# Norm outputs transposed by SyncE DMA, a state chain with one step per chunk, one pre-added LayerNorm sum, x and out on SyncE, and the last column half per token tile

## The chip, the cores and the metric

The kernel runs on the 8 cores of one Trainium2 chip. Each core works on 2 of the 16 sequences; nothing is exchanged between cores. The metric is the device time of the slowest core in microseconds (us). Engine names: PE is TensorE (matmul), DVE is VectorE, ACT is ScalarE, POOL is GpSimd, SP is SyncE, which here only issues DMAs.

## The reference

One decoder layer on 2064 tokens a sequence (16 meta tokens, then 2048), width 1024, feed-forward width 2816:

```
u = rms_norm(h) @ w_in                  # conv value 512, conv gate 512, q 256, k 256, v 512, out-gate 512, low rank 16
v = c_val * sigmoid(c_gate);  y = causal depthwise conv of v (width 31) + b
y_conv = silu(layer_norm over the 512 channels(y))
log_a = logsigmoid(lr @ w_gate2 + b) / 16;  bc = cumsum of log_a in a chunk
scores = tril((q e^bc) (k e^-bc)^T);  kv = (k e^(b_last - bc))^T v
state = e^b_last * state + kv                              # one step per chunk
o = scores v + (q e^bc) state_before;  y_gla = rms_norm per head(o) * silu(g)
h = h + concat(y_conv, y_gla) @ w_out
h = h + (silu(n @ w_gate) * (n @ w_up)) @ w_down           # n = rms_norm(h)
out = rms_norm(h), meta positions dropped
```

## The kernel before

**Blocks and stages.** A core's 4096 tokens are 8 blocks of 512, each of 4 token tiles of 128. A block goes through `mixer` (norm, projections, conv, attention, w_out, second norm) and `ffn` (22 pairs j of gate and up matmuls, two column halves of 6 down steps, the final norm). The mixer of block b+1 is merged into the ffn of block b, so the program is: mixer 0 alone (with a pass over the meta tokens), seven merged stages, ffn 7 alone. In this document a stage starts with the first matmul on `x2T` of an ffn; that moment is called T0.

**Norm and transposition.** `norm` (L554) writes a normed tile to one of two buffers `xn_tm` [128 tokens x 1024]: an ACT Square with a sum (L557), eight small DVE instructions (L525 to L534) and one DVE multiplication (L560). `transp` (L565) turns it to channel-major form: 8 PE transpositions of 128x128 into one PSUM bank (L572) and one ACT copy (L575) to `xT` (for the mixer) or `x2T` (for the ffn). The next norm into the same `xn_tm` waits for these transpositions.

**LayerNorm sums.** The mean over 512 channels is 4 fp32 matmuls with a matrix of ones (L744), the sum of squares 4 bf16 ones (L750). The difference and product that apply it are POOL instructions (L864, L865).

**State.** For each of the 4 chunks of a block POOL writes two halves of `Rbd` from the state `S` (L940), then DVE computes `U` (L946, 2 instructions) and the new `S` (L950, 2).

**Weights.** 48 tiles [128 x 2048]. At its first use a tile is loaded and cast from fp32 by a POOL DMA (`wring<-wpack`, L420), and SP stores the bf16 copy (`wsc<-wring`, L421); later uses load that copy on SP (`wring<-wsc`, L417). Slots wring0 to wring3 serve the mixer, wring4 to wring7 the ffn. A slot's next load is issued once PE has used the tile in it. The shifted copies for the conv (`rep<-vT`, L679) are 32 SP DMAs a block. x and the meta tile are loaded, and out is stored, by POOL DMAs (L457, L459, L601, L1130). `h` has two sets of 4 tiles; the load of x into a set waits until the out DMA of the block two before has read it.

**The order.** `Prog.add` records every instruction with its buffers; `Prog.schedule` (L139) simulates the engines with the costs of `Meter` and one DMA channel of rate `DMA_RATE`, and emits each engine's list in that order. An engine, and SP's and POOL's queue too, then runs its list in order: what waits holds everything behind it.

## Time and profile before

| | us |
|---|---|
| median of 3 runs (1739.64 to 1741.36) | 1740.09 |
| the profiled execution | 1738.95 |
| its slowest core, first to last instruction (span) | 1737.4 |
| spans of the 8 cores | 1726.5 to 1737.4 |
| PE busy | 1538.3 (89%) |
| DVE, ACT, POOL busy | 845.8, 526.2, 192.9 |
| mean granted TensorE clock, this core | 0.963 |

The profiled execution is 1.55 us longer than its span, and 1.1 us below the median. By the window table the span falls into 174 us of mixer 0 (PE busy for 95.6), the first merged stage from 174 to 400 (its weights are loaded for the first time), six stages of 195 to 197 us, and ffn 7 with the end. Matmul durations in rows are longer than the interval at which they follow each other, because they are pipelined: the start times of rows tell the interval.

### The profile page before, as it was taken

The numbers are of one execution on the slowest core, as the hardware profiler recorded it, in microseconds if no ns is written. First come the engines' busy times: TensorE is split into PE (matmuls) and PEld (weight loads), VectorE is DVE, ScalarE is ACT, GpSimd is POOL, SyncE is SP. The second block draws the span as 40 slices with busy tenths as digits, with TensorE's granted clock in tenths as the row PEclk, the third lists the DMA queues.
The fourth block names the chain that finished last, engine by engine and source line by source line (L and its number), as shares of the span: only waits on it lengthen the run. The fifth ranks groups of instructions, "written<-read, shape, count | busy, mean of one in ns | idle before, by whom it ended". The sixth has DMA issues, their size and how long they took to land.

```text
span 1737.4 us, 27522 instructions; the slowest of 8 cores (1726.5 to 1737.4 us)
## 1 busy us (share of the span) xinstructions
PE 1538.3 (89%) x8498; PEld 711.8 (41%) x8498; DVE 845.8 (49%) x1950; ACT 526.2 (30%) x822; POOL 192.9 (11%) x262
## 2 busy tenths in 40 slices
PE   1676997878899989999899989999899989999993
PEld 1332443433344434444444434444444434444431
DVE  4246427603427554466427554466427554466322
ACT  2233343201342234313342234313342234313101
POOL 2040013001002000200012000200002000200000
PEclk9897999999999999999999999999999999999997
DMA  9963786798353474445654475435653464434541
GB/s 211 230 150 98 160 194 153 171 213 272 103 147 122 169 220 144 150 144 165 193 156 122 169 218 142 153 134 174 196 154 122 170 218 144 151 122 140 176 145 73
DMA packets 93487, 281.92 MB, mean 162 GB/s; under 512 B 12576, under 2 KB 29344, under 8 KB 93344
## 3 DMA queue, kind: packets, MB, share of 16 engines
q1 hardware_dynamic: 76928, 220.84, 40.0%
q0 software_dynamic: 16416, 59.32, 15.5%
q8 instruction: 72, 1.18, 0.3%
q14 instruction: 71, 0.58, 0.1%
HBM read 245.70 MB, written 41.94 MB: 166 GB/s over the span
## 4 chain that ended last, share of the span: by engine, by line
PE 73%; DVE 8%; DMA 7%; issue 6%; ACT 2%; SPq 2%; DVEq 1%; POOL 0%; ACTq 0%; POOLq 0%
PE ps L581 49%; PE ps L1106 14%; PE ps L726 3%; DMA h_0<-xin 2%; DMA wring<-wpack 2%; PE ps L572 2%; SPq L679 2%; PE ps L744 2%; DVE xn_tm L560 1%; DMA wsc<-wring 1%; PE ps L639 1%; DVE y_tm L1000 1%; DVE stn L532 1%; DMA h_3<-pre 1%; DVE stn L534 1%
## 5 line engine op out<-in xcount | busy, mean ns | idle before, releaser
L581 PE MATMUL ps<-x2T,wring 128*128 128x512 bf16 x2816 | 646.7, 387 | 19.8 <-DVE ftmp L1088 9.1
L581 PEld LDWEIGHTS ps<-x2T,wring 128*128 128x128 bf16 x2816 | 274.8, 100 | 365.2 <-issue 62.0
L1106 PE MATMUL ps<-wring,actT 128*128 128x512 bf16 x1408 | 319.8, 382 | 20.5 <-DMA wring<-wpack 9.7
L1088 DVE SCALAR_TENSOR_TENSOR ftmp<-ftmp,ps 128x512 f32<-128x512 f32 x176 | 120.1, 686 | 257.1 <-ACT ftmp L1087 250.7
L1106 PEld LDWEIGHTS ps<-wring,actT 128*128 128x128 bf16 x1408 | 135.9, 98 | 182.2 <-issue 30.6
L1087 ACT ACTIVATE ftmp<-ps 128x512 f32<-128x512 f32 x176 | 104.7, 595 | 288.8 <-PE ps L581 232.8
L581 PE MATMUL ps<-xT,wring 128*128 128x512 bf16 x768 | 171.7, 380 | 2.6 <-DVE vT L668 1.1
L1090 DVE SCALAR_TENSOR_TENSOR actT<-ftmp,ps 128x512 bf16<-128x512 f32 x176 | 119.7, 686 | 74.7 <-PE ps L581 70.8
L581 PE MATMUL ps<-wring,xT 128*128 128x512 bf16 x512 | 120.2, 386 | 2.8 <-ACT actT L712 1.4
L581 PE MATMUL ps<-wring,yT 128*128 128x512 bf16 x512 | 118.6, 382 | 2.7 <-ACT yT L1015 2.7
L572 PE MATMUL ps<-ident,xn_tm 128*128 128x128 bf16 x520 | 45.6, 239 | 80.8 <-DVE stn L525 38.7
L581 PEld LDWEIGHTS ps<-xT,wring 128*128 128x128 bf16 x768 | 74.7, 98 | 92.1 <-issue 4.6
L940 POOL TENSOR_TENSOR Rbd<-S,emid 64x256 bf16<-64x256 f32 x64 | 43.0, 671 | 473.7 <-ACT emid L781 345.1
L572 PEld LDWEIGHTS ps<-ident,xn_tm 128*128 128x128 bf16 x520 | 36.9, 107 | 100.1 <-issue 94.1
L581 PEld LDWEIGHTS ps<-wring,xT 128*128 128x128 bf16 x512 | 50.3, 99 | 65.9 <-issue 9.8
L581 PEld LDWEIGHTS ps<-wring,yT 128*128 128x128 bf16 x512 | 49.9, 98 | 61.9 <-issue 4.7
L1114 DVE TENSOR_TENSOR h_0<-h_0,ps 128x512 f32<-128x512 f32 x16 | 11.0, 688 | 124.7 <-PE ps L1106 124.7
L1130 POOL DMA_DIRECT2D out<-h_0 x8 | 4.7, 588 | 554.4 <-DVE h_0 L1127 554.4
L672 DVE SCALAR_TENSOR_TENSOR vT<-mtmp,ps 128x512 bf16<-128x512 f32 x32 | 22.0, 688 | 81.5 <-issue 49.1
L726 PE MATMUL ps<-rep,wcv 128*32 128x512 bf16 x1024 | 59.3, 380 | 0.5 <-issue 0.2
L575 ACT ACTIVATE x2T<-ps 128x1024 bf16<-128x1024 bf16 x32 | 32.4, 1023 | 83.2 <-PE ps L572 80.4
L970 ACT ACTIVATE sg<-ps 128x512 f32<-128x512 f32 x32 | 19.1, 597 | 126.5 <-PE ps L581 90.8
(181 smaller groups left out, 1383.0 us busy)
## 6 DMA issues: line engine op xcount, KB each, us to landing
wring<-wsc SPq DMA_DIRECT2D x336, 512.0 KB, 4.3
wring<-wpack POOLq DMA_DIRECT2D x48, 512.0 KB, 9.5
wsc<-wring SPq DMA_DIRECT2D x48, 512.0 KB, 6.9
rep<-vT SPq DMA_DIRECT2D x256, 67.5 KB, 3.4
h_0<-xin POOLq DMA_DIRECT2D x8, 512.0 KB, 12.5
h_1<-xin POOLq DMA_DIRECT2D x8, 512.0 KB, 10.3
h_2<-xin POOLq DMA_DIRECT2D x8, 512.0 KB, 11.5
h_3<-xin POOLq DMA_DIRECT2D x8, 512.0 KB, 12.5
```

Of the source, the lines that this page charges most:

```text
L572: ins = e.transpose(out=ptb[:, kc, :], in_=xn_tm[i][:, kc * 128:(kc + 1) * 128], identity=ident[:])
L575: P.add("act", lambda e: e.activation(out=dst, in_=ptb, func=AF.Copy), R=[Bpt], W=[Bdst])
L581: ins = e.matmul(pt_ap, lhsT=lhs(kc), rhs=rhs(kc), start=(kc == 0), stop=(kc == KC - 1))
L672: P.add("dve", lambda e, pv=pv, th=th: e.scalar_tensor_tensor(out=vT[:, c, 32:32 + T], in0=th[:], scalar=1.0, in1=pv[:], op0=ALU.add, op1= ...
L679: P.add("sp", lambda e, s_=s_, g=g, c0=c - 1: e.dma_start(out=rep[s_ * 32:(s_ + 1) * 32, c0:c0 + 2, g, :], in_=vT[g * 32:(g + 1) * 32, c0: ...
L726: ins = e.matmul(pcv[g * 32:(g + 1) * 32, :], lhsT=wcv[:, c, g, a, :], rhs=rep[:, c, g, 4 * a:4 * a + T], start=(a == 0), stop=(a == 7))
L744: ins = e.matmul(p1[:], lhsT=ones[:], rhs=ycv[c], start=(c == 0), stop=(c == 3))
L940: P.add("pool", lambda e, t=t, hh=hh, rows=rows: e.tensor_tensor(out=Rbd[rows, t, :, hh, :], in0=S[rows, :, :], in1=em2[rows, :, t].unsque ...
L1087: P.add("act", lambda e: e.activation(out=th[:], in_=pg[:], func=AF.Tanh, scale=0.5), R=[Bpg], W=[Bth])
L1088: P.add("dve", lambda e: e.scalar_tensor_tensor(out=th[:], in0=th[:], scalar=1.0, in1=pg[:], op0=ALU.add, op1=ALU.mult), R=[Bpg, Bth], W=[ ...
L1090: P.add("dve", lambda e: e.scalar_tensor_tensor(out=actT[:, j, :], in0=th[:], scalar=0.5, in1=pu[:], op0=ALU.mult, op1=ALU.mult), R=[Bpu, ...
L1106: ins = e.matmul(ps[t][:], lhsT=actT[:, j, t * 128:(t + 1) * 128], rhs=wd3[:, j - 4 * s_, :], start=(j == 0), stop=(j == NJ - 1))
```

## The change

- `transp` becomes one SP instruction, `dma_start_transpose` from `xn_tm` to `xT` or `x2T` (now laid out tile by tile); the PE transpositions, their PSUM bank and the ACT copy go.
- The LayerNorm mean: three POOL additions, then one fp32 matmul.
- The state: `S` has 5 slots; 4 multiplications (two halves at once) and 8 chained steps on DVE, then the 8 `Rbd` writes. The cumulative sums are 8 scans of 128 in place of 2 of 512.
- x, meta tile and out move from POOL's queue to SP's; the first four mixer weights are issued after x tiles 0 and 3 have landed; two gain vectors are loaded later.
- The down steps are one entry per token tile; in the last ffn the second column half runs token tile by token tile, each with its final norm and store, and 4 of its 6 weights lie in the mixer's slots.
- The planner's DMA rate goes from 185e3 to 380e3 bytes per us with a latency of 3.0 in place of 2.0. It sets no hardware, but moves instructions on every engine.

```diff
-DMA_RATE = 185e3
+DMA_RATE, DMA_LAT = 380e3, 3.0
...
+            if name == "dma_start_transpose":
+                self.nbytes += n * o.shape[0] * 3
+                self.cost += 0.5
...
-                end = dma_free + 2.0
+                end = dma_free + DMA_LAT
...
-            P.add("pool", lambda e: e.dma_start(out=h[1][3][:], in_=pre_d), W=[Bh[1][3]], dkey="h1_3")
+            P.add("sp", lambda e: e.dma_start(out=h[1][3][:], in_=pre_d), W=[Bh[1][3]], dkey="h1_3")
             for t in range(NT):
-                P.add("pool", lambda e, t=t: e.dma_start(out=h[0][t][:], in_=xin[t * 128:(t + 1) * 128, :]),
+                P.add("sp", lambda e, t=t: e.dma_start(out=h[0][t][:], in_=xin[t * 128:(t + 1) * 128, :]),
...
-                        wissue(r, n)
+                        wissue(r, n, [Bh[0][0]] if r == 0 and n < 2 else [Bh[0][3]] if r == 0 else [BxT[3]])
...
             def transp(i, dst, Bdst):
-                pt, Bpt = mps()
-                ptb = pt[:].bitcast(BF16).rearrange("p (k n) -> p k n", k=KC)
-
-                def tr(e):
-                    ins = None
-                    for kc in range(KC):
-                        ins = e.transpose(out=ptb[:, kc, :], in_=xn_tm[i][:, kc * 128:(kc + 1) * 128], identity=ident[:])
-                    return ins
-                P.add("pe", tr, R=[Bxn[i], Bident], W=[Bpt])
-                P.add("act", lambda e: e.activation(out=dst, in_=ptb, func=AF.Copy), R=[Bpt], W=[Bdst])
+                P.add("sp", lambda e: e.dma_start_transpose(dst, xn_tm[i][:]), R=[Bxn[i]], W=[Bdst], dkey=f"xt{i}")
...
-                            P.add("pool", lambda e, t=t: e.dma_start(out=h[hs][t][:], in_=xin[row0 + t * 128:row0 + (t + 1) * 128, :]),
+                            P.add("sp", lambda e, t=t: e.dma_start(out=h[hs][t][:], in_=xin[row0 + t * 128:row0 + (t + 1) * 128, :]),
...
-                    def mm1(e):
-                        ins = None
-                        for c in range(4):
-                            ins = e.matmul(p1[:], lhsT=ones[:], rhs=ycv[c], start=(c == 0), stop=(c == 3))
-                        return ins
...
+                    P.add("pool", lambda e: e.tensor_tensor(out=mu[:], in0=ycv[0], in1=ycv[1], op=ALU.add), R=Bycv[0:2], W=[Bmu])
+                    P.add("pool", lambda e: e.tensor_tensor(out=rs[:], in0=ycv[2], in1=ycv[3], op=ALU.add), R=Bycv[2:4], W=[Brs_])
+                    P.add("pool", lambda e: e.tensor_tensor(out=mu[:], in0=mu[:], in1=rs[:], op=ALU.add), R=[Brs_], W=[Bmu])
+                    P.add("pe", lambda e: e.matmul(p1[:], lhsT=ones[:], rhs=mu[:], start=True, stop=True), R=[Bmu, Bc], W=[Bp1])
+                    P.add("pe", mm2, R=Bysq + [Bc], W=[Bp2])
...
+                        sp4 = sp.rearrange("p a (t n) -> p (a t) n", n=128)
+                        for i in range(2 * nt):
+                            P.add("dve", lambda e, i=i: e.tensor_tensor_scan(
+                                out=cs4[:, i, :], data0=ones[:], data1=sp4[:, i, :], initial=0.0,
...
+                    el = csb[:].rearrange("p a (t n) -> p a t n", n=128)[:, :, :, 127]
+                    P.add("dve", lambda e: e.tensor_tensor(out=dec[:], in0=em2, in1=el, op=ALU.mult), R=[Bemid, Bcs], W=[Bdec])
+                    for t in range(NT):
+                        P.add("dve", lambda e, t=t: e.tensor_tensor(
+                            out=S[:, sl[t + 1]], in0=pkv[t // 2][0][:, (t % 2) * 256:(t % 2) * 256 + 256].rearrange(
+                                "p (a n) -> p a n", a=2), in1=el[:, :, t].unsqueeze(2).to_broadcast([128, 2, 128]), op=ALU.mult),
+                            R=[Bcs, pkv[t // 2][1]], W=[BS[sl[t + 1]]])
+                    for t in range(NT):
+                        for hp in range(2):
+                            P.add("dve", lambda e, t=t, hp=hp: e.scalar_tensor_tensor(
+                                out=S[:, sl[t + 1], hp, :], in0=S[:, sl[t], hp, :], scalar=dec[:, hp, t:t + 1],
+                                in1=S[:, sl[t + 1], hp, :], op0=ALU.mult, op1=ALU.add), R=[BS[sl[t]], Bdec], W=[BS[sl[t + 1]]])
                     for t in range(NT):
                         for hh in range(2):
                             rows = slice(hh * 64, (hh + 1) * 64)
                             P.add("pool", lambda e, t=t, hh=hh, rows=rows: e.tensor_tensor(
-                                out=Rbd[rows, t, :, hh, :], in0=S[rows, :, :],
+                                out=Rbd[rows, t, :, hh, :], in0=S[rows, sl[t], :, :],
                                 in1=em2[rows, :, t].unsqueeze(2).to_broadcast([64, 2, 128]), op=ALU.mult),
-                                R=[BS, Bemid], W=[BR[t]])
-                        for hp in range(2):
-                            o = (t % 2) * 256 + hp * 128
-                            P.add("dve", lambda e, t=t, hp=hp, o=o: e.scalar_tensor_tensor(
-                                out=U[:, hp, :], in0=S[:, hp, :], scalar=em2[:, hp, t:t + 1], in1=pkv[t // 2][0][:, o:o + 128],
-                                op0=ALU.mult, op1=ALU.add), R=[BS, Bemid, pkv[t // 2][1]], W=[BU])
-                        for hp in range(2):
-                            P.add("dve", lambda e, t=t, hp=hp: e.tensor_scalar(
-                                out=S[:, hp, :], in0=U[:, hp, :], scalar1=csb[:, hp, t * 128 + 127:t * 128 + 128], scalar2=None,
-                                op0=ALU.mult), R=[BU, Bcs], W=[BS])
...
+                def down_mm(e, wd, t, js, j0):
+                    wd3 = wd[:].rearrange("p (j n) -> p j n", j=4)
+                    ins = None
+                    for j in js:
+                        ins = e.matmul(ps[t][:], lhsT=actT[:, j, t * 128:(t + 1) * 128], rhs=wd3[:, j - j0, :],
+                                       start=(j == 0), stop=(j == NJ - 1))
+                    return ins
...
+                            for t in range(NT):
+                                P.add("pe", lambda e, t=t: down_mm(e, wd, t, js_of(s_), 4 * s_),
+                                      R=[Bwd] + [Bact[j] for j in js_of(s_)], W=[Bps[t]])
+                                if s_ == 5:
...
+                def stat(t):
+                    i = nxt("xn", 2)
+                    P.add("act", lambda e: e.activation(out=xn_tm[i][:], in_=h[hs][t][:], func=AF.Square, accum_out=stf[:, 0, t:t + 1]),
+                          R=[Bh[hs][t]], W=[Bxn[i], Bstf[t]])
+
+                def finish(t0, t1):
+                    y = newton_row([stf[:, k, t0:t1] for k in range(6)], Bstf[t0:t1], 1.0 / D, RMS_EPS)
+                    for t in range(t0, t1):
+                        ht, Bht = h[hs][t], Bh[hs][t]
+                        P.add("dve", lambda e, t=t, ht=ht: e.scalar_tensor_tensor(
+                            out=ht[:], in0=ht[:], scalar=y[:, t - t0:t - t0 + 1], in1=gfin[:], op0=ALU.mult, op1=ALU.mult),
+                            R=[Bht, Bstf[t], Bgain[id(gfin)]], W=[Bht])
+                        P.add("sp", lambda e, t=t, ht=ht: e.dma_start(out=out[orow0 + t * 128:orow0 + (t + 1) * 128, :], in_=ht[:]),
+                              R=[Bht], dkey=f"h{hs}_{t}")
 
                 def final():
                     for t in range(NT):
+                        stat(t)
+                    finish(0, NT)
+
+                def down_last():
+
+                    wds = [wget(W_FD + 6 + s_, r=0 if s_ < NWM else 1)[0] for s_ in range(6)]
                     for t in range(NT):
+                        for s_ in range(6):
+                            wd, Bwd = wds[s_]
+                            P.add("pe", lambda e, t=t, s_=s_, wd=wd: down_mm(e, wd, t, js_of(s_), 4 * s_),
+                                  R=[Bwd] + [Bact[j] for j in js_of(s_)], W=[Bps[t]])
+                        h_add(1, t)
+                        stat(t)
+                        finish(t, t + 1)
+                units.append((19.0, down_last) if last else (0.0, final))
```

PE, the rows before the first projection of a stage, where `xn_tm` 0 and 1 are the normed tiles, `ps0` to `ps3` the ffn's PSUM banks and `ps4` to `ps7` the mixer's. Before:

```order
L581 MATMUL ps3<-x2T,wring7 128x512 x8
L581 MATMUL ps0<-x2T,wring4 128x512 x8
L581 MATMUL ps2<-x2T,wring4 128x512 x8
L572 MATMUL ps7<-ident,xn_tm1 128x128 x8
L581 MATMUL ps1<-x2T,wring5 128x512 x8
L581 MATMUL ps3<-x2T,wring5 128x512 x8
L572 MATMUL ps4<-ident,xn_tm0 128x128 x8
L581 MATMUL ps0<-x2T,wring6 128x512 x8
L581 MATMUL ps5<-xT,wring0 128x512 x8
```

PE at the same place now, from the last down steps of the ffn before to the low-rank projection (buffer numbers left out):

```order
L1093 MATMUL ps<-wring,actT 128x512 x40
L572 MATMUL ps<-x2T,wring 128x512 x216
L572 MATMUL ps<-xT,wring 128x512 x64
L626 MATMUL ps<-xT,wgl 32x512 x8
L572 MATMUL ps<-x2T,wring 128x512 x8
```

The eight groups of transpositions of a stage are gone from PE's list (four stood between these x2T matmuls, four in the w_out part); in most stages 216 matmuls on x2T now stand ahead of the first one on xT.

POOL, the out stores and the x loads of a stage (`h1_0` to `h1_3` are the four tiles of one set). Before:

```order
L1130 DMA out<-h1_2 128x1024 [waits sem_dve]
L1130 DMA out<-h1_3 128x1024 [waits sem_dve]
L601 DMA h1_0<-xin 128x1024 [waits dsem_h1_0]
L601 DMA h1_1<-xin 128x1024 [waits dsem_h1_1]
L601 DMA h1_2<-xin 128x1024 [waits dsem_h1_2]
L601 DMA h1_3<-xin 128x1024 [waits dsem_h1_3]
L940 TENSOR_TENSOR Rbd<-S,emid 64x2x128 [waits sem_act,sem_pool,sem_pe]
```

SP at this place now (`dsem_h1_0` is the store of that tile, `sem_pe` a tile used, `sem_dve` the end of a DVE instruction):

```order
L1126 DMA out<-h1_3 128x1024 [waits sem_dve]
L420 DMA wring6<-wsc 128x2048 [waits dsem_wh6,sem_pe]
L595 DMA h1_0<-xin 128x1024 [waits dsem_h1_0]
L595 DMA h1_1<-xin 128x1024 [waits dsem_h1_1]
L420 DMA wring7<-wsc 128x2048 [waits dsem_wh7,sem_pe]
L595 DMA h1_2<-xin 128x1024 [waits dsem_h1_2]
L595 DMA h1_3<-xin 128x1024 [waits dsem_h1_3]
L420 DMA wring4<-wsc 128x2048 [waits dsem_wh4,sem_pe]
L420 DMA wring5<-wsc 128x2048 [waits dsem_wh5,sem_pe]
L566 DMA_TRANSPOSE xT<-xn_tm1 128x8x128 [waits sem_dve,dsem_xt1]
```

The stores, loads and transposes now stand in one list with the ffn's weight loads. Between the four transposes of xT stand the weights of one pair each, so that the second, third and fourth come after a pair of loads that waits for PE.

SP at the start of the program (wring4 to wring7 hold the first ffn weights, `actT` receives the meta tile here). Before:

```order
L448 DMA gng<-gla_norm_g 128x1
L421 DMA wsc<-wring0 128x2048 [waits dsem_wp0]
L421 DMA wsc<-wring1 128x2048 [waits dsem_wp1]
L421 DMA wsc<-wring2 128x2048 [waits dsem_wp2]
L679 DMA rep<-vT 32x2x540 [waits sem_dve]
```

Now:

```order
L424 DMA wsc<-wring4 128x2048 [waits dsem_wp4]
...
L424 DMA wsc<-wring7 128x2048 [waits dsem_wp7]
L566 DMA_TRANSPOSE actT<-xn_tm0 128x8x128 [waits sem_dve]
L595 DMA h1_3<-xin 128x1024 [waits dsem_h1_3,sem_act]
L566 DMA_TRANSPOSE xT<-xn_tm1 128x8x128 [waits sem_dve]
L424 DMA wsc<-wring0 128x2048 [waits dsem_wp0]
...
L424 DMA wsc<-wring3 128x2048 [waits dsem_wp3]
L566 DMA_TRANSPOSE xT<-xn_tm0 128x8x128 [waits sem_dve]
```

The first transposes stand behind the stores of wring4 to wring7, the transposes of tiles 1 to 3 also behind those of wring0 to wring3, and each store waits for its fp32 load.

## Rows read from the trace of the kernel before

**Rows 1.** Window table: the first merged stage and a later one.

```profile
core 1: us, PE busy (x) PEld busy (x) DVE busy (x) ACT busy (x) POOL busy (x), PEclk, DMA share, GB/s
174.00:400.00 226.00, 193.84 (x1040) 87.82 (x1038) 92.62 (x215) 59.07 (x91) 32.52 (x47) 0.96 0.79 181
889.00:1084.00 195.00, 187.33 (x1028) 86.94 (x1030) 103.76 (x239) 64.62 (x101) 20.49 (x25) 0.98 0.51 162
```

**Rows 2.** Groups of one stage (885 to 1081 us): busy, mean ns | idle before, releaser.

```profile
L572 PE MATMUL ps<-ident,xn_tm 128*128 128x128 bf16 x64 | 5.7, 241 | 4.5 <-DVE stn L525 4.2 <-DVE xn_tm L560 0.2
...
L864 POOL TENSOR_TENSOR rep<-rep,mtmp 128x512 f32<-128x512 f32 x4 | 5.1, 1270 | 17.1 <-PE ps L750 16.7
...
L575 ACT ACTIVATE x2T<-ps 128x1024 bf16<-128x1024 bf16 x4 | 4.1, 1022 | 12.2 <-PE ps L572 12.2
L744 PE MATMUL ps<-rep,ones 128*128 128x512 f32 x8 | 3.6, 592 | 0.0
...
L946 DVE SCALAR_TENSOR_TENSOR U<-S,emid,ps 128x128 f32<-128x128 f32 x8 | 2.8, 344 | 0.9 <-PE ps L931 0.4
```

**Rows 3.** Timeline of PE, start of a stage: start us, us, instruction [idle before].

```profile
1001.37 13.97 PE L581 MATMUL ps<-x2T,wring 128*128 128x512 bf16 x64 [0.94 <-DVE h_0 L1114]
...
1034.34 1.01 PE L572 MATMUL ps<-ident,xn_tm 128*128 128x128 bf16 x8 [4.20 <-DVE stn L525]
1035.15 3.62 PE L581 MATMUL ps<-x2T,wring 128*128 128x512 bf16 x8
...
1055.03 13.98 PE L581 MATMUL ps<-xT,wring 128*128 128x512 bf16 x64
```

**Rows 4.** Timeline of PE, end of the stage before that.

```profile
990.10 1.25 PE L572 MATMUL ps<-ident,xn_tm 128*128 128x128 bf16 x16
...
998.09 0.61 PE L572 MATMUL ps<-ident,xn_tm 128*128 128x128 bf16 x8
998.54 1.89 PE L1106 MATMUL ps<-wring,actT 128*128 128x512 bf16 x8
```

**Rows 5.** Timeline of DVE there: the last normed tile for x2T.

```profile
994.94 1.28 DVE L560 SCALAR_TENSOR_TENSOR xn_tm<-h_3,stn,gffn 128x1024 bf16<-128x1024 f32 x1
```

**Rows 6.** Timeline of POOL, the first store of out in that stage.

```profile
1012.42 0.60 POOL L1130 DMA_DIRECT2D out<-h_0  x1 [69.96 <-DVE h_0 L1127]
```

**Rows 7.** DMA issues of the program: queue, count, KB, median us to landing.

```profile
wring<-wsc SPq DMA_DIRECT2D x336, 512.0 KB, 4.3
...
wsc<-wring SPq DMA_DIRECT2D x48, 512.0 KB, 6.9
rep<-vT SPq DMA_DIRECT2D x256, 67.5 KB, 3.4
h_0<-xin POOLq DMA_DIRECT2D x8, 512.0 KB, 12.5
...
out<-h_0 POOLq DMA_DIRECT2D x8, 512.0 KB, 4.2
...
out<-h_3 POOLq DMA_DIRECT2D x8, 512.0 KB, 9.6
```

**Rows 8.** Timelines of PE (first transposition), SP and ACT at the program's start.

```profile
20.11 1.01 PE L572 MATMUL ps<-ident,xn_tm 128*128 128x128 bf16 x8 [20.11 <-DVE stn L525]
...
25.80 7.11 SPq L421 DMA_DIRECT2D wsc<-wring  x3
...
41.52 1.02 ACT L575 ACTIVATE xT<-ps 128x1024 bf16<-128x1024 bf16 x1 [2.28 <-PE ps L572]
```

**Rows 9.** Timelines of PE, ACT, DVE and POOL at the program's end.

```profile
1688.05 20.84 PE L1106 MATMUL ps<-wring,actT 128*128 128x512 bf16 x88 [2.73 <-DVE h_3 L1114]
...
1713.57 1.06 ACT L1121 ACTIVATE xn_tm<-h_3 128x1024 bf16<-128x1024 f32 x1
...
1717.26 1.28 DVE L1127 SCALAR_TENSOR_TENSOR h_0<-h_0,stf,gfin 128x1024 f32<-128x1024 f32 x1
...
1722.95 0.54 POOL L1130 DMA_DIRECT2D out<-h_3  x1 [0.92 <-DVE h_3 L1127]
```

More of the change, by code:

```diff
@@ L352, in build @@
             Bst = [Buf(f"st{i}") for i in range(2 * NT)]
-            Bstf = Buf("stf")
+            Bstf = [Buf(f"stf{t}") for t in range(NT)]
             Bsto = [Buf(f"sto{i}") for i in range(2)]
@@ L583, in mm8, with mixer @@
                 return f
-            def mixer(hs, row0, first, meta, load):
+            def mixer(bi, row0, first, meta, load):
+                hs = bi % 2
                 units = []
+                s0 = (NT * bi) % (NT + 1)
+                sl = [(s0 + i) % (NT + 1) for i in range(NT + 1)]
                 def unit(cost):
@@ L1066, in _, with ffn @@
                     def _(t=t):
-                        transp(xni2[t], x2T[:, :, t * 128:(t + 1) * 128], Bx2T[t])
+                        transp(xni2[t], x2T[:, t], Bx2T[t])
                 return units
-            def ffn(hs, orow0):
+            def ffn(hs, orow0, last):
                 units = []
```

163 lines of the change are left out of this document (66 added, 97 removed).

## Prediction

> **What bounds the kernel now.** I read the busy shares by window first [rows 1], then the groups of one stage [rows 2], then PE's timeline at both ends of a stage [rows 3, 4], the DMA issues [rows 7], and the program's two ends [rows 8, 9]. In a later stage PE is busy for 187.33 of 195 us and DVE for 103.76: PE is the bound, and only 7.7 us are waits. A matmul of 128x512 counts 0.216 us there: 64 of them take 13.98 and 8 take 1.89, and the 56 between cost 12.09 [rows 3, 4]. The largest wait, 4.20 us, stands before the first transposition to xT [rows 3]. So a stage gets shorter by what leaves PE's list and by that wait, as long as no transfer that takes their place is late. The first merged stage is another matter: 226 us with 32 idle, DMA engines busy for .79 of it [rows 1], because weights are read in fp32 and written back there.
>
> The profiled execution took 1738.95 us (span 1737.4 and 1.55 outside), 1.1 below the median. I sum against 1738.95 and add the 1.1 at the end.
>
> **What a stage loses.** Transpositions: eight groups of 8. The one of 1034.34 is followed by x2T matmuls at 1035.15, so it takes 0.81 [rows 3]; the one of 998.09 takes 0.45 [rows 4]. Two of the first kind and six of the second: 4.3 us. The 4.20 us wait goes with them [rows 3]. LayerNorm mean: the group of eight fp32 records is 3.6 us for four matmuls [rows 2] (each is two passes); one in place of four leaves a quarter, which saves 2.6. Together 11.1 us of 195.
>
> **What a stage gains in waits.** All of them hang on L, the time from a transpose's issue on SP to its landing. No row of before shows a transpose by DMA. The nearest rows are SP's own: 3.4 us for 67.5 KB, 4.3 for a weight load of 512 KB, 6.9 for a store of 512 KB; out's slowest store takes 9.6 and x's slowest load 12.5, both on POOL's queue [rows 7]. A transposed tile is 256 KB from SBUF to SBUF on SP, so I take 4.3, with 3.4 and 6.9 as likely ends and 12.5 as the far one.
>
> - x2T. The last tile for it is normed at 994.94 + 1.28 = 996.22 [rows 5]; the transposition before it, whose two groups stand after the last w_out matmul, began at 990.10 [rows 4], 6.1 earlier. By the order now only 40 down matmuls, 8.6 us, stand between w_out and x2T. PE waits 6.1 + 0.1 (issue) + L - 8.6 = L - 2.4, which is 1.9 us. Before, the last 8 down matmuls ended at 998.54 + 8 x 0.216 = 1000.27 and x2T began at 1001.37: 1.1 [rows 3, 4]. Cost 0.8.
> - xT. In the order now 216 x2T matmuls precede the first on xT, so it is due at T0 + 46.7; before it was T0 + 53.7 (1055.03 less 1001.37). The last of the four transposes stands on SP behind a pair of weights whose slots come free when the sixth pair has been used, at 6 x 32 x 0.216 = T0 + 41.5. It lands at about T0 + 41.9 + L = 46.2; with L = 6.9 PE waits 2.1. I take 1.
> - Weights. SP runs its list in order. The load of wring7 now stands behind a load of x, which waits until the store of the same tile has landed. Stores begin about T0 + 11 (1012.42 less 1001.37) [rows 6], the second a DVE instruction later, T0 + 12.2, and land 4.2 to 9.6 later [rows 7]. The weights are next needed at T0 + 13.8 plus a load's slack: a pair feeds 32 matmuls, 6.9 us, and a load takes 4.3, which leaves 2.6, and one pair is held ahead. That gives 0 to 3.7 us of idle PE there, and up to 0.9 more at the load behind the fourth x. I take 2, of 0 to 4.6. On POOL the same waits held no weights.
>
> The other edits I cost at nothing. Three POOL additions of 1.27 us (L864) [rows 2] stand before the LayerNorm matmul, but x2T matmuls of the merged ffn fill PE meanwhile; without that cover about 2.6 us a stage. The state chain on DVE drops the U instructions (eight of 344 ns [rows 2]) for twelve of such size, on an engine 53% busy; uncovered, 1.4 us. The ACT copies of 1.02 us [rows 2] go from an engine that is a third busy. The planner's new rate sets no hardware; what it moves is in the three orders above, and was counted.
>
> So a later stage nets 11.1 - 0.8 - 1 - 2 = 7.3 us, and six of them 44. In the first merged stage the fp32 loads set much of the pace; I give it 4 (0 to 11).
>
> **The end.** PE ended at 1688.05 + 20.84 = 1708.89, the span at 1737.4: 28.5 us [rows 9]. The final norm's first multiplication started 8.4 us after PE, at 1717.26, behind four Squares of 1.06, and the last store was issued at 1722.95 [rows 9]. Now one tile is left: 8.4 less three Squares, 5.2; the multiplication 1.28; one store of 4.2 to 9.6 [rows 7], and about 1 to finish: 12 to 17, where I take 14.5, a gain of 14. The 2.73 us wait between the column halves [rows 9] should lose some 2. Together 16 (11 to 19).
>
> **The start.** Before, the first transposition ran at 20.11 and xT was complete at 41.52 + 1.02 = 42.5 [rows 8]. Now SP holds the first transposes behind the stores of wring4 to wring7, and tiles 1 to 3 also behind those of wring0 to wring3. The first three stores were issued from 25.80 to 32.91 [rows 8], about 3.6 apart; eight at this pace end at 50.6. With x ahead of the weights and L behind, xT is complete at 44 to 56: a loss of 1.5 to 13. Part of it returns, since mixer 0 is not PE's to set. I take 3 lost, of 8 gained to 13 lost.
>
> Sum: 44 + 4 + 16 - 3 = 61, so 1738.95 - 61 = 1678, on the scale of the medians **1679 us**. Own range: 1655 to 1705, from L at 3.4 with no weight late, to L = 5.5 with 3 us of late weights a stage and 9 us lost at the start.
>
> **The rivals.**
>
> *All of it is covered* (L = 3.4 or less, no weight late). Seven stages give 11.1 each, 78; the end 19, the start -1.5: 95 less, 1645. For it: one pair of weights is held ahead, and the DMA share of a later stage is only .51 [rows 1]. Against it: the four SP lists above put waits in front of loads that were free of them.
>
> *SP's queue eats the gain.* With L = 6.9 x2T costs 4.5 - 1.1 = 3.4, xT 2.1, weights 4.6: a stage keeps 11.1 - 10.1 = 1. Seven of these, the end 11, the start -11: 7 less, 1733. For it: SP now carries 16 DMAs a stage more, and its stores take 6.9 [rows 7]. Moving x and out alone then bought nothing. An x load of 512 KB took 12.5 us on POOL's queue, a weight load of that size 4.3 on SP's [rows 7], but they ran in different company. The Trainium skill ("DMA: Bandwidth & Descriptors", section "Issuing engines are not separate DMA queues") says that DMAs of all engines end up on the same 16 DMA engines, and that the choice of issuer saves only the time of issuing; by that rule x stays at 12.5 on SP. No run here shows it yet.
>
> *Slower: the transposes land late.* The mechanism is at the stage's start. Only two xn_tm buffers exist, so the third norm waits for the first transpose to land; tiles follow each other in 24 matmuls, 5.2 us, so above that L counts twice: x2T costs (L - 2.4) + (L - 5.2) - 1.1, xT L - 4.8, weights 2. At L = 9.6, the slowest store [rows 7], that is 10.5 + 4.8 + 2 = 17.3 against 11.1: each of seven stages is 6.2 longer, 43; the ends give back 13; 30 more, 1770. It decides from L of about 8. For it: a transpose moves 2-byte elements in a pattern that no row shows. Against it: 256 KB is half of every tile in the rows. The Trainium skill ("VectorE: DVE Perf Modes", section "The three transpose paths") gives 1309 ns for a DMA transposition of 128x128 against 390 on TensorE; eight in a row would be an estimate of 10.5 us for L, and by the same formula about 1788. TensorE's eight took 0.45 to 0.81 us here [rows 3, 4], far below eight times 390, since they are pipelined; how far a DMA's are, no row here shows.
>
> **How the numbers follow.** Chances: the forecast .52, all covered .20, gain eaten .18, slower .10. A difference under 0.2%, 3.5 us, can't be told from none. The forecast and "all covered" are faster by more; of "gain eaten" about .10 is faster, .05 within the bound, and .03 slower, which with the last rival makes faster .82, same .05, slower .13. The range of 8 in 10 leaves out little at either side: 1643 to 1735.
>
> **What would show it.** The landing time of the transposes (4.3); PE's waits before the first x2T matmul (1.9) and the first xT matmul (0 to 2) of a stage, and before the x2T matmuls of the second and third pair (2); a later stage of about 188 us with no 4.2 us wait; an end of 14.5 us after PE; xT of mixer 0 complete at 44 to 56. The forecast is wrong if the transposes take over 6 us, if PE waits over 5 us a stage for a weight tile behind an out store, or if the POOL additions show up as a wait before the LayerNorm matmul.

## The result, and the profile after

The changed kernel takes 1668.34 us (median; before 1740.72 beside it), a ratio of 0.9590, 95% interval 0.9560 to 0.9619. The forecast was 1679, so the size and the sign came out. Most of the reasons did not: the largest single gain belongs to an edit that the prediction priced at nothing, and the edit that it was built on, the transposes by DMA, costs time in the whole.

The profiled execution took 1674.6 us (span 1673.1 on core 0); the one of before 1738.95 (core 1). Executions of the changed kernel scatter more than those of before, over 9 us (1665.61 to 1674.6) against 2, and the profiled one is the longest of its four. Both spans, cut where an ffn begins (T0: the first matmul on x2T):

| stretch | before | after | difference | forecast |
|---|---|---|---|---|
| mixer 0, to the first T0 | 173.9 | 202.6 | +28.7 | +3 |
| first merged stage | 229.1 | 202.0 | -27.0 | -4 |
| second | 207.2 | 190.6 | -16.6 | -7.3 |
| five later ones | 977.8 | 945.2 | -32.6 (6.5 each) | -36.5 (7.3 each) |
| last T0 to the end | 149.5 | 132.7 | -16.8 | -16 |

The later stages and the end came in sum as worked out. The start lost ten times its term, and the first two merged stages, where little was expected, returned all of it and 15 us more. The second merged stage of before had been counted ahead of the prediction among the six of 195 to 197 us; it took 207.2.

PE's timeline of after (start us, us, instruction, idle before), at the starts of the program, of the first and the second ffn, and of a later stage; it answers to [rows 3, 4, 8]:

```profile
54.37 5.28 PE L572 MATMUL ps<-actT,wring 128*128 128x128 bf16 x48 [54.37 <-DMA actT<-xn_tm]
71.01 12.00 PE L572 MATMUL ps<-xT,wring 128*128 128x512 bf16 x48 [11.36 <-DMA xT<-xn_tm]
...
202.58 12.77 PE L572 MATMUL ps<-x2T,wring 128*128 128x512 bf16 x48 [18.57 <-DMA x2T<-xn_tm]
...
404.62 12.44 PE L572 MATMUL ps<-x2T,wring 128*128 128x512 bf16 x48 [3.94 <-DMA x2T<-xn_tm]
...
784.45 12.25 PE L572 MATMUL ps<-x2T,wring 128*128 128x512 bf16 x56 [1.90 <-DMA x2T<-xn_tm]
797.41 10.52 PE L572 MATMUL ps<-x2T,wring 128*128 128x512 bf16 x48 [0.72 <-DVE actT L1079]
811.33 18.87 PE L572 MATMUL ps<-x2T,wring 128*128 128x512 bf16 x79 [3.40 <-DMA wring<-wsc]
```

In the later stage PE waits 1.90 us for x2T (forecast 1.9), nothing for xT (forecast 1), and 3.40 for a weight tile (forecast 0 to 4.6). At the program's start the first matmul waits until 54.37 and the first on xT runs at 71.01, where before it ran at 42.69; the first ffn then waits 18.57 for its x2T.

The window table of that stage against the later one of [rows 1] (columns as there), and the DMA issues that answer to [rows 7]:

```profile
784.45:973.20 188.75, 180.57 (x971) 81.98 (x980) 104.19 (x242) 57.64 (x93) 20.10 (x20) 0.99 0.62 180
```

```profile
wring<-wsc SPq DMA_DIRECT2D x336, 512.0 KB, 4.5
...
h_0<-xin SPq DMA_DIRECT2D x8, 512.0 KB, 7.4
...
h_3<-xin SPq DMA_DIRECT2D x8, 512.0 KB, 10.5
out<-h_0 SPq DMA_DIRECT2D x8, 512.0 KB, 5.8
...
xT<-xn_tm SPq DMA_TRANSPOSE x32, 5.1
...
x2T<-xn_tm SPq DMA_TRANSPOSE x32, 4.2
...
actT<-xn_tm SPq DMA_TRANSPOSE x1, 18.9
```

L, which no row of before showed, is 4.2 and 5.1 us in the median, where 4.3 was taken. But the meta tile's transpose at the start took 18.9.

### The profile page after: what moved, and what is told of

It reads as the page before. It is cut to its first block, busy times and chain, and to the rows that moved or that the text cites. A ratio compares the mean times of both kernels' runs of the same rounds, so it can differ in the third digit from the quotient of the medians.

```text
span 1673.1 us, 26740 instructions; the slowest of 8 cores (1636.5 to 1673.1 us)
## 1 busy us (share of the span) xinstructions
PE 1473.3 (88%) x7864; PEld 670.7 (40%) x7930; DVE 853.4 (51%) x1998; ACT 464.8 (28%) x757; POOL 189.8 (11%) x221
## 4 chain that ended last, share of the span: by engine, by line
PE 68%; DMA 13%; DVE 8%; issue 5%; SPq 3%; ACT 1%; DVEq 0%; POOL 0%; ACTq 0%; POOLq 0%
PE ps L572 51%; PE ps L1093 11%; PE ps L720 3%; DMA wring<-wpack 2%; DMA x2T<-xn_tm 2%; DMA out<-h_1 2%; SPq L673 2%; DMA wring<-wsc 2%; DVE y_tm L989 1%; DMA actT<-xn_tm 1%; DMA h_1<-xin 1%; DVE xn_tm L560 1%; PE ps L633 1%; DMA rep<-vT 1%; DVE sto L984 1%
## 5 line engine op out<-in xcount | busy, mean ns | idle before, releaser
L1093 PE MATMUL ps<-wring,actT 128*128 128x512 bf16 x1382 | 315.3, 380 | 5.5 <-DMA wring<-wpack 4.2
L572 PEld LDWEIGHTS ps<-xT,wring 128*128 128x128 bf16 x768 | 75.0, 98 | 104.9 <-issue 16.6
L572 PE MATMUL ps<-actT,wring 128*128 128x128 bf16 x80 | 8.1, 284 | 66.6 <-DMA actT<-xn_tm 54.4
L423 POOL DMA_DIRECT2D wring<-wpack x48 | 26.1, 546 | 279.0 <-PE ps L572 170.8
L656 ACT ACTIVATE mtmp<-ps 128x512 f32<-128x512 f32 (+1 forms) x36 | 20.2, 561 | 99.7 <-PE ps L572 86.6
L557 ACT ACTIVATE xn_tm<-h_0 128x1024 bf16<-128x1024 f32 x16 | 16.9, 1056 | 107.3 <-DVE h_0 L1045 87.6
L989 DVE SCALAR_TENSOR_TENSOR y_tm<-ps,sto,sg 128x128 bf16<-128x128 f32 x128 | 42.0, 349 | 8.1 <-DVE sto L550 0.4
## 6 DMA issues: line engine op xcount, KB each, us to landing
h_3<-xin SPq DMA_DIRECT2D x8, 512.0 KB, 10.5
```

What stands on the lines that cost most here:

```text
L423: P.add("pool", lambda e: e.dma_start(out=dst, in_=wpack[tile]), R=after, W=[B_], dkey=f"wp{sl}")
L572: ins = e.matmul(pt_ap, lhsT=lhs(kc), rhs=rhs(kc), start=(kc == 0), stop=(kc == KC - 1))
L656: P.add("act", lambda e, pg=pg, th=th, n=n: e.activation(out=th[:, 0:n], in_=pg[:, 0:n], func=AF.Tanh, scale=0.5), R=[Bpg], W=[Bth])
L989: P.add("dve", lambda e, hd=hd, hsl=hsl: e.scalar_tensor_tensor(out=y_tm[i][:, hsl], in0=po[:, hsl], scalar=y[:, hd:hd + 1], in1=sg[i][:, ...
L1093: ins = e.matmul(ps[t][:], lhsT=actT[:, j, t * 128:(t + 1) * 128], rhs=wd3[:, j - j0, :], start=(j == 0), stop=(j == NJ - 1))
```

## The experiments

All ratios are to the kernel before on the same chip; "us" behind a ratio is the ratio times 1740.7. By this the changed kernel is at 1669.

### e1: the planner's numbers alone

```diff
-DMA_RATE = 185e3
+DMA_RATE, DMA_LAT = 380e3, 3.0
-                self.nbytes += n * o.shape[0] * (2 if kw["in_"].dtype == BF16 else 4)
+                self.nbytes += n * o.shape[0] * (2 if kw["in_"].dtype == BF16 else (4 if o.dtype == F32 else 5.4))
-                end = dma_free + 2.0
+                end = dma_free + DMA_LAT
```

> The kernel before with only the planner's new numbers (rate 380e3, latency 3.0, bytes of a cast load). Theory A (the gain of a later stage comes from what leaves PE's list: transpositions, their wait, three fp32 matmuls): the six later stages stay at 195 us, all within 5 us of 1740.7. Theory B (the gain comes from the order that the new numbers make): stages of about 189, some 1700 or below.

0.9681 (0.9658 to 0.9705), 1685 us: three quarters of the whole gain, with no instruction added or removed. Theory B was right on the sum and wrong on the place: T0 stood at 176.0, 368.1 and 561.5 on core 0, so the first merged stage took 192.1 us (229.1 before) and the second 193.4 (207.2), while five later stages averaged 195.0 (195.6 before; over all eight cores 192.6 and 195.1). How this comes about is read at the end of the first merged stage. First PE of the kernel before, from 385 us on, then PE of e1 from 335 us on:

```profile
385.90 3.61 PE L1106 MATMUL ps<-wring,actT 128*128 128x512 bf16 x16 [2.48 <-DMA wring<-wpack]
390.32 3.61 PE L1106 MATMUL ps<-wring,actT 128*128 128x512 bf16 x16 [0.80 <-DMA wring<-wpack]
394.19 3.61 PE L1106 MATMUL ps<-wring,actT 128*128 128x512 bf16 x16 [0.26 <-DMA wring<-wpack]
400.03 1.89 PE L1106 MATMUL ps<-wring,actT 128*128 128x512 bf16 x8 [2.22 <-DMA wring<-wpack]
```

```profile
335.30 1.89 PE L1106 MATMUL ps<-wring,actT 128*128 128x512 bf16 x8
337.03 3.62 PE L581 MATMUL ps<-wring,yT 128*128 128x512 bf16 x16
340.48 3.62 PE L1106 MATMUL ps<-wring,actT 128*128 128x512 bf16 x16
343.94 1.89 PE L581 MATMUL ps<-wring,yT 128*128 128x512 bf16 x8
345.66 3.62 PE L1106 MATMUL ps<-wring,actT 128*128 128x512 bf16 x16
```

Before, only down steps (L1106) are left, and each waits for its fp32 weight tile; the mixer's work is used up. In e1 w_out (yT) and down steps alternate, and none waits. The window tables, before and e1, of the two ends and of the whole first merged stage:

```profile
350.00:402.90 52.90, 39.53 (x170) 16.25 (x169) 3.29 (x6) 0.60 (x2) 4.23 (x8) 0.97 1.00 228
174.00:402.90 228.90, 195.72 (x1048) 88.54 (x1047) 93.43 (x217) 59.09 (x92) 32.52 (x47) 0.96 0.80 184
```

```profile
330.00:368.00 38.00, 36.76 (x200) 17.57 (x197) 18.04 (x46) 9.62 (x14) 2.12 (x4) 1.00 1.00 249
176.00:368.00 192.00, 187.50 (x1048) 86.91 (x1048) 94.81 (x217) 59.52 (x91) 32.40 (x47) 0.99 0.94 221
```

At both ends the DMA engines are full (1.00). Before, PE was busy for 39.5 of 52.9 us and DVE for 3.3; in e1 36.8 of 38.0 and 18.0. In the order made for the lower rate the w_out matmuls ran from 302 to 326 us and the down steps came last; in e1 w_out runs from 326 to 356, between them. Over the whole stage the DMA engines were busy for 0.80 of the time before and 0.94 in e1, and the last fp32 tile landed at 399.9 and at 359.1.

The end is not all of the 37 us. PE was idle for 33.2 us of the stage before, in e1 for 4.6. Of the 33.2 us 9.7 were waits for fp32 tiles, the others mostly waits of 1 to 3 us for the mixer's own steps on DVE, which e1's order covers. The remaining 8 us are PE's busy time (195.7 and 187.5), for the same matmuls at a mean granted clock of 0.96 and 0.99. In the second merged stage no fp32 tile is left to load; there idle time fell from 15.9 to 7.3 us. That the moved order is the cause follows from the run, since nothing else differs; which of the three numbers did it was not tried.

### e2: TensorE's transpositions back; e6: the transposes by DMA alone on e1

e2 is the changed kernel with the eight PE transpositions and the ACT copy of a tile again; e6 is e1 with the transposes by DMA.

```diff
-                P.add("sp", lambda e: e.dma_start_transpose(dst, xn_tm[i][:]), R=[Bxn[i]], W=[Bdst], dkey=f"xt{i}")
+                P.add("pe", tr, R=[Bxn[i], Bident], W=[Bpt])
+                P.add("act", lambda e: e.activation(out=dst, in_=ptb, func=AF.Copy), R=[Bpt], W=[Bdst])
```

> The changed kernel with the norm outputs transposed by TensorE and copied by ACT again, everything else as changed. Theory A: a later stage is 4.3 us longer by the transpositions and 1 to 4 by the wait before those of xT, less the 2 us wait for x2T, so 189 becomes 193 to 196, and the whole 1668 plus 7 x 3 to 7, 1690 to 1717. Theory B: the order pays, not the transposes: 1668 within 5. The start should be shorter (no transposes behind stores on SP), with T0 of the first ffn some 20 us earlier than 202; if that is worth its length, the sum is 20 less.

> The kernel before with the planner's new numbers (as e1) and the transposes by DMA, nothing else. If the transposes by DMA are a loss in sum as e2 says (about 17 us): 1700 to 1710 beside e1's 1687, with the first T0 at 195 to 205 against 176. If they shorten a later stage by what leaves PE (4.3 us and the waits): later stages 187 to 190 against e1's 195, first T0 late all the same, 1665 to 1685.

e2: 0.9485 (0.9470 to 0.9500), 1651 us, 18 less than the changed kernel: both theories missed, since without the part that was to bring the gain the kernel is faster. e6: 0.9857 (0.9838 to 0.9877), 1716 us, 31 more than e1: undoing the edit and doing it alone agree in sign. On the slowest core e6 has its first T0 at 211.3 (e1 176.0) and a first merged stage of 206.6 (192.1); its five later stages average 191.9 (195.0). So the transposes by DMA give 3 us in a later stage of that kernel (over eight cores 4.2: 188.4 for 192.6) and lose 50 in the first two stretches. In the first merged stage PE of the changed kernel waits 11.6 us for fp32 weight tiles and 3.9 for x2T; in e2, with TensorE's transpositions, it waits for neither DMA there, and the stage takes 188.3 us for 202.0. PE of e2 at the start and in a later stage:

```profile
45.92 1.01 PE L572 MATMUL ps<-ident,xn_tm 128*128 128x128 bf16 x8 [15.13 <-DVE cvec L507]
...
64.37 5.83 PE L581 MATMUL ps<-xT,wring 128*128 128x512 bf16 x18 [1.49 <-ACT xT L575]
...
761.51 13.98 PE L581 MATMUL ps<-x2T,wring 128*128 128x512 bf16 x64
775.78 13.97 PE L581 MATMUL ps<-x2T,wring 128*128 128x512 bf16 x64 [0.30 <-DVE ftmp L1086]
792.13 1.89 PE L581 MATMUL ps<-x2T,wring 128*128 128x512 bf16 x8 [2.38 <-DMA wring<-wsc]
793.86 0.61 PE L572 MATMUL ps<-ident,xn_tm 128*128 128x128 bf16 x8
794.30 3.62 PE L581 MATMUL ps<-x2T,wring 128*128 128x512 bf16 x16
```

At the start its first matmul on xT runs at 64.37, also late: the second group of transpositions waits 15.13 us for DVE, which waits for small constants (read below, at e3). In the later stage a transposition takes 0.44 us and nothing waits ahead of it: the 4.20 of [rows 3] is gone with PE's transpositions in place, and a wait of 2.38 stands before, at a weight tile. There is no wait for x2T. Its five later stages average 189.4 us on core 0, after's 189.0; over the eight cores 188.4 and 187.0, a difference no larger than that between two profiles of the same PE order (see e8).

### e3 and e5: another start

```diff
+            gain(gmix, g_mix_d, "gm")           # and the small constants: ahead of x on SP
...
-                        wissue(r, n, [Bh[0][0]] if r == 0 and n < 2 else [Bh[0][3]] if r == 0 else [BxT[3]])
+                    wissue(0, n, [Bh[0][0]] if n < 2 else [Bh[0][3]])
...
+                if i == 1 + NT and wseq is not None:      # after the transposes of xT of block 0
+                    for f_ in late:                       # the first four bf16 stores
+                        f_([BxT[3]])
+                    for n in range(RING[1][1]):           # the first ffn weights
+                        wissue(1, n, [BxT[3]])
```

The changed kernel makes the loads of the ffn weights depend on the last tile of xT, but at that place of the program nothing has written it yet, so that no wait arises and these four are the first weights to be loaded. Here they come after xT.

> The changed kernel with another start: the small constants and gmix before x on SP, the loads of wring4 to wring7 and the first bf16 stores after the four transposes of the first xT. Theory A (the 28.7 us that the first ffn starts later are lost time): T0 of the first ffn at 175 to 185 instead of 202, and the whole 1640 to 1650. Theory C (the first loads of the weights, fp32 with their stores, set when the second ffn can start, so the late start is given back): T0 of the second ffn stays at 395 to 405, and the whole is 1660 to 1670.

> TensorE's transpositions as in e2, and the other start of e3: constants and gmix before x on SP, the loads of wring4 to wring7 and the first bf16 stores after the first xT. With TensorE's transpositions nothing of the first xT stands behind those stores, so T0 of the first ffn should be 173 to 178 (e1: 176; e2: 190). Theory A (a late start is lost time): the second T0 at 362 to 368 and the whole 12 to 14 below e2, 1638 to 1640. Theory C (the first loads of the weights set the second T0): it stays at 375 to 380, the whole at 1648 to 1653.

e3, with transposes by DMA: 0.9585 (0.9543 to 0.9628), no difference from the changed kernel; neither theory was tested, for T0 stayed at 203.7. e5, with TensorE's: 0.9404 (0.9386 to 0.9423), 1637 us, 14 less than e2; T0 172.8 to 179.1 on the eight cores, the second at 361 to 371. It beats both kernels: 6.0% below before, 1.9% below the change. Theory A holds: a late start is lost time, as soon as it can be mended. With the transposes by DMA this start did not mend it. SP of the changed kernel, at the start:

```profile
19.87 15.42 SPq L424 DMA_DIRECT2D wsc<-wring  x4
35.38 14.70 SPq L566 DMA_TRANSPOSE actT<-xn_tm  x1
50.25 0.45 SPq L595 DMA_DIRECT2D h_3<-xin  x1
50.79 2.44 SPq L566 DMA_TRANSPOSE xT<-xn_tm  x1
53.32 3.19 SPq L424 DMA_DIRECT2D wsc<-wring  x4
```

Until 35.29 SP waits for the four fp32 loads, as forecast; but then it is held for 14.70 us by the issue of one transpose (1.2 us in a later stage), while the DMA engines are full (busy for all of the time from 35 to 54 us). DVE at the same time:

```profile
25.90 1.28 DVE L560 SCALAR_TENSOR_TENSOR xn_tm<-h_3,stn,gmix 128x1024 bf16<-128x1024 f32 x1 [14.34 <-DMA gmix<-norm_mix_g]
...
44.30 0.17 DVE L505 TENSOR_SCALAR gb<-gb 128x2 f32<-128x2 f32 x1 [17.12 <-DMA gng<-gla_norm_g]
44.48 1.28 DVE L560 SCALAR_TENSOR_TENSOR xn_tm<-h_0,stn,gmix 128x1024 bf16<-128x1024 f32 x1
```

gmix and a constant of half a KB, now issued behind x, hold DVE until 25.9 and 44.3. In e3, freed of both, SP is held by the first transpose for less long (17.75 to 23.40), and PE starts at 37.18 and on xT at 53.34, 17.7 us earlier than in the changed kernel. That T0 does not come earlier has another cause. DVE and PE of e3:

```profile
92.71 0.19 DVE L664 SCALAR_TENSOR_TENSOR vT<-mtmp,ps 128x32 bf16<-128x32 f32 x1 [25.33 <-DMA rep<-vT]
93.04 1.01 PE L574 MATMUL ps<-actT,wring 128*128 128x128 bf16 x8 [22.40 <-DVE vT L664]
```

The copies for the conv stand behind the fp32 loads and bf16 stores that were moved there, and PE waits 22.40 us for them, and 5.23 once more later in mixer 0; in the changed kernel it is 11.55 and no second wait. Before T0 it then waits 17.92 us for x2T (18.57 in the changed kernel). e5 has the wait behind the copies too, 24.18 us, but its first matmul on xT runs at 33.67 and its wait for x2T is 1.26.

### e4: x and out on POOL's queue again

```diff
-                            P.add("sp", lambda e, t=t: e.dma_start(out=h[hs][t][:], in_=xin[...
+                            P.add("pool", lambda e, t=t: e.dma_start(out=h[hs][t][:], in_=xin[...
```

(and the same for the meta tile, the first x and out).

> The changed kernel with x, the meta tile and out on POOL's queue again. Theory A: the wait for weights behind an x load (2.9 to 3.4 us a stage on the slowest core) goes, later stages 186 to 187, the whole some 15 less, 1653, as long as nothing on POOL waits for x or out. Rival: POOL's queue holds LayerNorm's additions or the fp32 weight loads behind the out stores, and a stage grows by 2 to 5: 1680 to 1700. Rule that the issuing engine does not matter: within 5 of 1668.

0.9625 (0.9597 to 0.9654) against 0.9590 (0.9560 to 0.9619): 6 us more, the intervals touch. Theory A falls: with x off SP's list PE still waits 1 to 3 us at the same place of a later stage (1.06, 1.38 and 1.08 in one, 3.17 in the next); over eight cores its five later stages average 187.1 us, after's 187.0. Most of the 6 us stands at the end: the issue of the last store is 8.0 us from the end of the span on SP, 13.0 on POOL.

```profile
1665.14 0.33 SPq L1126 DMA_DIRECT2D out<-h_3  x1
```

```profile
1662.86 0.54 POOL L1126 DMA_DIRECT2D out<-h  x1 [2.24 <-DVE h L1123]
```

The first row is of the changed kernel (span 1673.1), the second of e4 (1675.9). The store itself lands 2.6 us after its issue in the first and 2.9 in the second. What differs comes behind it, the DRAIN that stands last in POOL's list (count, then shortest/median/longest in ns):

```profile
L1168 POOLq DRAIN  x1: 4057/4057/4057, 1668.8 to 1668.8; - x1
```

```profile
L1168 POOLq DRAIN  x1: 8876/8876/8876, 1666.8 to 1666.8; - x1
```

It takes 8.88 us in the four kernels whose x and out are POOL's (before, e1, e4, e6: 114 DMAs in POOL's list) and 4.06 in the ten where they are SP's (49), on every core. Why is not shown.

### e7, e8 and e9: the LayerNorm mean, the end and the state chain taken back

```diff
-                    P.add("pe", lambda e: e.matmul(p1[:], lhsT=ones[:], rhs=mu[:], start=True, stop=True), R=[Bmu, Bc], W=[Bp1])
+                    P.add("pe", mm1, R=Bycv + [Bc], W=[Bp1])     # four matmuls; the POOL additions go
```
```diff
-                f = ffn(b % 2, blocks[b][0], b == nb - 1)
+                f = ffn(b % 2, blocks[b][0], False)
```
```diff
-  out=S[t+1] = pkv * el (4 instructions);  S[t+1] = S[t] * dec + S[t+1] (8)
+  S[t+1] = S[t] * em2 + pkv (8);  S[t+1] = S[t+1] * el (8)
```

The first two are excerpts of edits of the changed kernel; the third, in short, is of an edit of e5.

> The changed kernel with the LayerNorm mean as four fp32 matmuls again, without the three POOL additions. By the prediction's term a later stage is 2.6 us longer (189 becomes 191.6 on the slowest core) and the whole 18 longer, 1686. If the merged ffn's matmuls had hidden them, or POOL's additions cost a wait of their own: within 5 of 1668.

> The changed kernel with the last ffn's second column half in six steps over all token tiles, one final norm, four stores at the end, as before the change. By the prediction's term the time from the last T0 to the end is 16 us longer (132.7 becomes 149) and the whole 1684. Rival: the token tile order had its gain from SP's stores alone, then 5 to 8 longer, 1675.

> e5 with the state chain in two dependent DVE steps a chunk as before the change (16 steps and no multiplications ahead, in place of 4 multiplications, one product and 8 steps). The prediction cost this edit at nothing: then 1638 within 4. If the chain is on the path of a stage, each chunk adds a step of 0.34 us and its semaphore, some 1.5 us a stage: 1645 to 1652.

e7: 0.9708 (0.9654 to 0.9762), 21 us more than the changed kernel where 18 were forecast, and by its interval 11 to 30; the term stands as to its size. Over eight cores and five later stages PE is busy for 2.4 us more a stage, where 2.6 was taken, and the stage is 1.7 longer; mixer 0 and the first merged stage are 3 longer each. e8: 0.9585 (0.9543 to 0.9626), no difference that these runs can tell; in its profile the time from the last T0 is 134.7 us (after 132.7, before 149.5), and PE's end is 19.7 us from the span's (after 16.0, before 28.5). So of the 12.5 us gained behind PE's end 3.7 are the token tile order and 4.8 the shorter DRAIN, which e8 has too; the other 4.0 were not taken apart. e8 also gives a measure of chance: in the five later stages its matmuls stand in the changed kernel's order, yet these stages average 184.9 us over eight cores in its profile and 187.0 in after's. e9: 0.9395 (0.9376 to 0.9414) against e5's 0.9404 (0.9386 to 0.9423): the chain makes no difference that these runs can tell, as forecast.

### e10, e11 and e12: what is left in a later stage

```diff
-                plan += merge(f, m, 0.15, 0.93) if m else [fn for _, fn in f]
+                plan += merge(f, m, 0.2, 0.93) if m else [fn for _, fn in f]
```
```diff
+                if bi >= 2:
+                    P.add("sp", lambda e: e.dma_start_transpose(dst, xn_tm[i][:]), R=[Bxn[i]], W=[Bdst], dkey=f"xt{i}")
+                    return
```
```diff
-                end = dma_free + DMA_LAT
+                end = dma_free + DMA_LAT + getattr(o, "late", 0.0)      # 6.0 for the loads of x
```

All three start from e5.

> e5 with the next block's mixer beginning in the ffn at 20% of its planned time instead of 15%. Theory X (the wait of 2 to 3.7 us in the first 32 us of a stage is x arriving late: the norm waits for x at the head of DVE's list, and the ffn's own DVE steps behind it hold PE's banks): the wait goes and a later stage is 185 to 186, the whole 1615 to 1625. Theory W (it is the weights' load behind x on SP): the wait stays where it is, and the whole is 1638 within 5, or longer, since the mixer is pressed into less time.

> e5 with the transposes by DMA from block 2 on, and by TensorE for the meta tile and blocks 0 and 1. If the transposes by DMA lose only at the start and in the first merged stage (e6 against e1) and save 1 to 4 us in a later one: later stages 184 to 187 against e5's 185 to 190, and the whole 1615 to 1632. If what they save is given back by PE's wait for x2T (2 us) and by SP's list: 1638 within 5; a longer time would say that they cost in every stage.

> e5, where the planner alone takes the loads of x as landing 6 us later than it did (4.4 after issue by its own numbers, against 7.4 to 10.5 in the profiles), so that it puts the norm of x behind more of the ffn's steps on ACT and DVE; no load is moved by hand. In e10 the norm still stood in the same place of ACT's list and waited 4.0 us for x, with the ffn's tanh behind it. Theory X (that wait is PE's wait of 2 to 3.7 us in the first 35 us of a stage): it goes, a later stage is 2 to 3 us shorter than e5's 185 to 190, the whole 1617 to 1627. Theory W (PE waits there for a weight tile whose load is late on SP or in the DMA engines): the wait for a weight tile stays, 1638 within 5.

e10: 0.9406 (0.9384 to 0.9429); e11: 0.9418 (0.9400 to 0.9436); e12: 0.9411 (0.9395 to 0.9427): none differs from e5. e11 isolates the transposes in a later stage, free of the start. PE there:

```profile
753.57 13.93 PE L586 MATMUL ps<-x2T,wring 128*128 128x512 bf16 x56 [2.94 <-DMA x2T<-xn_tm]
768.21 8.79 PE L586 MATMUL ps<-x2T,wring 128*128 128x512 bf16 x40 [0.71 <-DVE actT L1093]
...
780.92 4.26 PE L586 MATMUL ps<-x2T,wring 128*128 128x512 bf16 x19 [1.69 <-DMA wring<-wsc]
```

Most of the 4 us of transpositions have left PE's busy time, and 2.94 + 0.71 stand as waits at the start of the ffn instead. Over five later stages and eight cores PE is busy for 180.6 us in e11 and 183.4 in e5, and idle for 6.8 and 3.8; 2.3 of e11's idle time are waits for x2T. A stage averages 187.4 us in e11 and 187.2 in e5; the mean granted clock of its cores is 0.966 to 0.973, e5's 0.970 to 0.979.

e10 and e12 asked what PE's last wait in the first 35 us of a stage is. In e10 ACT waits there for x, and the ffn's DVE steps stand behind:

```profile
968.22 1.06 ACT L559 ACTIVATE xn_tm<-h 128x1024 bf16<-128x1024 f32 x1 [4.02 <-DMA h<-xin]
```

In e12 the norm stands later, and PE waits for a weight tile instead:

```profile
785.12 10.48 PE L583 MATMUL ps<-x2T,wring 128*128 128x512 bf16 x40 [2.00 <-DMA wring<-wsc]
```

Theory X falls as the whole cause: of five later stages on e12's slowest core two wait 2.0 and 2.2 us there for a weight tile, one 1.5 for DVE, two under 1, and a stage averages 187.7 us over eight cores, no less than e5's. From T0 + 10 to T0 + 30 four out stores, four loads of x and the weights of three pairs are issued, and the DMA engines are busy for 0.90 of the time (770 to 790 us of e12); whether they or SP's list set the wait stays open.

## Why the prediction was right, and where it was wrong

**The steps that held.** L (4.3 taken, 4.2 and 5.1 measured), the x2T wait (1.9 and 1.90; 2.3 over eight cores), the weights' wait (2 of 0 to 4.6; 3.4 in the stage shown, 1.4 over eight cores and five stages), the LayerNorm term (18 and 21 in all), the state chain at nothing (e9). The xT wait (1) came to nothing. A later stage became 6.5 us shorter where 7.3 was the sum (8.1 over eight cores); that the sum held is in part luck, since the planner alone gives 2.5 of the 8.1 (e1) and the transposes, which were to give most, between 4.2 and nothing (e6, e2, e11).

**The end.** 14.5 us after PE were forecast and 16.0 measured, with terms that offset each other: the last store landed in 2.6 us where 4.2 to 9.6 were taken, and from there to the end it was 5.3, most of it POOL's DRAIN, where "about 1 to finish" was taken.

**The planner's numbers.** The new rate "sets no hardware; what it moves is in the three orders above, and was counted": this step failed. The orders shown were those around the transposes; none was read at the end of the first merged stage, where the trace of before had the waits of [rows 1] (32 idle us of 226) in plain view. They were put down to the fp32 loads as such. e1 has the same loads, and PE of its slowest core waits for none of them in the first merged stage: another order is worth 37 and 14 us in the first two merged stages.

**The transposes.** "The 4.20 us wait goes with them" failed: e2 has the transpositions on PE and not this wait, and a wait remains near that place with them or without, for a weight tile or for DVE: 2.8 to 4.5 us in the five later stages of after's slowest core, 2.4 to 3.6 in e2's. What the transposes take from a later stage is 2.9 us of PE's busy time, and what they put in is the x2T wait and smaller ones, 3.0 in all: e11 finds no difference. At the start they cost 12 to 35 us of first T0 (e2 190.1, after 202.6; e1 176.0, e6 211.3).

**The start.** One mechanism was named, stores and loads ahead of the first transposes on SP, but the term was 3 us and the loss 28.7. Of this 16.2 stand in e2 too, whose transpositions are TensorE's (T0 at 190.1; 173.9 before): the part that was not counted at all is that gmix and the small constants now stand behind x and hold DVE. With them in front, and the ffn's weights and the first stores later, e5 is back at 174.5; the two were not tried apart. The other 12.5 come with the transposes (after 202.6). A transpose issued into full queues was given the L of a quiet one (18.9 us against 4.3), and mixer 0 has no other work for PE while x2T is made: from the end of its last w_out matmul to T0 it took 13.4 us before and takes 18.6 after, so that 5 of the 18.57 are new. There the slower rival's mechanism, two xn_tm buffers that the transposes must free, is seen: three of ACT's norms wait 16.5 us in all for transposes, 8.8 of it the norm of the third tile for this x2T.

**The rule of issuers.** By the Trainium skill ("DMA: Bandwidth & Descriptors", section "Issuing engines are not separate DMA queues") SP would save only the time of issuing. The whole agrees within what e4 can tell (6 us, intervals touching, 5 of them behind the last store). Single loads are shorter: x lands 7.4 to 10.5 us after its issue on SP and in the median 11.3 on POOL in e4, the same kernel but for this, where by the rule 12.5 was to stay; how much of that is time of issuing is not shown.

**The rule of transposes.** From the figure of the Trainium skill ("VectorE: DVE Perf Modes", section "The three transpose paths") the prediction had an estimate of 10.5 us for eight tiles by DMA. They landed in 4.2 to 5.1, so the measurement decides against the multiple. Its direction, TensorE the faster path, agrees: 0.44 to 0.81 us here, and 1.02 for ACT's copy. For the whole kernel it tells at the start and in the first merged stage (e2, e6), not in a later one (e11).

That 1668 lay near 1679 is thus the sum of two errors of opposite sign: 26 us too little loss at the start, 32 us too little gain in the two stages behind it. That they nearly cancel is luck.

## What to carry to other kernels

A number in a planner is an edit of every engine's list: read its order wherever the trace shows idle time, above all at the end of a stretch whose loads are full, and see what is left there to run beside them. Price a transfer by the queues it is issued into, not by its median, and look separately at the first pass, where there is nothing to hide it. When an edit and its tuning come together, run the tuning alone first: here it was worth 55 us, the transposes that it came with minus 18. At a program's end read what stands behind the last store, too: here 4 to 9 us of the span.
